# Gathering each expert unit's rows already transposed, with the normed tokens as matmul weights

## What is computed

```python
def grouped_moe(h, router_w, router_b, w_gate, w_up, w_down):
    aff = jax.nn.sigmoid((h @ router_w).astype(jnp.float32))
    ...
    _, idx = lax.top_k(jnp.where(in_group, biased, -jnp.inf), TOP_K)      # 2 of 16
    ...
    for e in range(N_EXPERTS):
        he = jax.nn.silu(h @ w_gate[e]) * (h @ w_up[e])
        y = y + combine[..., e:e + 1] * (he @ w_down[e])
    return y
```

## Time and profile before

| | before |
|---|---|
| median of 3 runs (lowest to highest) | 970.78 us (969.52 to 971.41) |
| profiled execution: span of the core | 969.1 us |
| mean granted TensorE clock in it | 0.906 |
| TensorE matmul busy | 807.4 us (83%) |
| VectorE busy | 405.9 us (42%) |
| ScalarE busy | 178.4 us (18%) |
| HBM read, written | 303.84 MB, 24.12 MB |

### The profile page before, as it was taken

How to read it: one execution, slowest core, us unless ns; L and a number is a source line. 1 busy time by engine, 2 the same in 40 slices (tenths; PEclk the granted TensorE clock), 3 DMA queues, 4 the chain that set the end, 5 groups by cost and what they waited for, 6 DMA issues and landing times.

```text
span 969.1 us, 18246 instructions
## 1 busy us (share of the span) xinstructions
PE 807.4 (83%) x6990; PEld 435.3 (45%) x6991; DVE 405.9 (42%) x944; ACT 178.4 (18%) x383; POOL 43.1 (4%) x71
## 2 busy tenths in 40 slices
PE   8899999997979856996668977799879879697674
PEld 3544646444554423553234543374445535353332
DVE  3267879867879841221011223533522111122315
ACT  3222010325630201111001110330211110111002
POOL 0100000130001010000000001000010000000010
PEclk9799989998999897998778989799899989798878
DMA  9989977999506797859999999994779999999971
GB/s 341 361 305 351 336 266 266 332 347 336 199 1 235 300 404 271 350 223 418 415 418 415 355 406 411 391 416 162 276 293 397 371 414 417 414 417 413 415 302 54
DMA packets 99192, 320.22 MB, mean 330 GB/s; under 512 B 10161, under 2 KB 24417, under 8 KB 82609
## 3 DMA queue, kind: packets, MB, share of 16 engines
q1 hardware_dynamic: 75648, 282.49, 74.3%
q0 software_dynamic: 4864, 22.03, 6.1%
q10 hardware_dynamic: 18624, 14.96, 4.7%
HBM read 303.84 MB, written 24.12 MB: 338 GB/s over the span
## 4 chain that ended last, share of the span: by engine, by line
PE 43%; DMA 25%; DVE 12%; SPq 11%; issue 4%; ACT 3%; ACTq 1%; POOL 1%; DVEq 0%; POOLq 0%
DMA raw<-in_w_up 10%; SPq L479 9%; DMA arena<-unit_rows 9%; PE bank L1824 9%; PE bank L1603 7%; PE bank L1837 4%; PE bank L1593 3%; PE bank L1745 3%; PE bank L1998 3%; PE bank L1607 2%; DMA consts_sb<-in_constants 2%; DMA unit_rows<-arena,row_i 2%; DMA arena<-ada_sums 1%; PE bank L1612 1%; PE bank L1539 1%
## 5 line engine op out<-in xcount | busy, mean ns | idle before, releaser
L1824 PE MATMUL bank<-raw,arena 128*32 128x256 f32 x3392 | 241.8, 428 | 65.2 <-DMA raw<-in_w_up 33.8
L1824 PEld LDWEIGHTS bank<-raw,arena 128*32 128x32 f32 x3392 | 118.0, 121 | 170.0 <-DMA raw<-in_w_up 46.9
L1369 DVE TENSOR_TENSOR arena<-arena,bank 64x256 f32<-64x256 f32 x53 | 22.5, 425 | 340.3 <-ACT arena L815 340.3
L1837 PE MATMUL bank<-raw,arena 128*32 128x256 f32 x1696 | 113.1, 397 | 10.2 <-DVE arena L1357 10.2
L1837 PEld LDWEIGHTS bank<-raw,arena 128*32 128x32 f32 x1696 | 59.6, 115 | 50.1 <-DVE arena L1357 11.1
L1603 PE MATMUL bank<-ring,arena 128*128 128x512 f32 x160 | 69.9, 594 | 0.0
L1811 PE MATMUL bank<-consts_sb,arena 64*128 64x64 f32 x212 | 36.5, 295 | 36.6 <-DVE arena L1369 36.5
L815 ACT ACTIVATE arena<-bank 64x256 f32<-64x256 f32 x53 | 19.9, 376 | 254.5 <-PE bank L1824 217.5
L928 DVE SCALAR_TENSOR_TENSOR bias<-ring,small,bias 128x512 f32<-128x512 f32 x77 | 57.9, 752 | 2.7
L1811 PEld LDWEIGHTS bank<-consts_sb,arena 64*128 64x128 f32 x212 | 29.0, 196 | 48.7 <-DVE arena L1369 41.7
L928 DVE SCALAR_TENSOR_TENSOR arena<-ring,small,arena 128x512 f32<-128x512 f32 x63 | 47.4, 752 | 2.2
(11 more groups left out here) (269 smaller groups left out, 856.4 us busy)
## 6 DMA issues: line engine op xcount, KB each, us to landing
raw<-in_w_gate SPq DMA_DIRECT2D x64, 1024.0 KB, 21.0
raw<-in_w_up SPq DMA_DIRECT2D x64, 1024.0 KB, 23.3
raw<-in_w_down SPq DMA_DIRECT2D x64, 1024.0 KB, 22.3
ring<-in_ada_w SPq DMA_DIRECT2D x24, 2048.0 KB, 13.0
ring<-in_w_in SPq DMA_DIRECT2D x7, 2048.0 KB, 13.2
unit_results<-arena ACTq DMA_DIRECT2D x220, 32.0 KB, 7.2
arena<-unit_rows ACTq DMA_DIRECT2D x55, 128.0 KB, 6.9
ring<-in_w_out SPq DMA_DIRECT2D x2, 2048.0 KB, 42.6
```

Source lines behind the costliest of these rows:

```text
L1824: ins = mm(ps[4][o:o + S, 0:FW], xT[:, i, j * S:(j + 1) * S], w[:, k % 4, h * FW:(h + 1) * FW], start=(k == 0), stop=(k == KD - 1))
L1837: ins = mm(ps[5][j * S:(j + 1) * S, 0:XW], hT_e[:, k % QN, k // QN * S:(k // QN + 1) * S], w[:, k % 2, j * XW:(j + 1) * XW], start=(k == 0 ...
```

## The change

For every unit, TensorE gathers the rows itself and already transposed: for each of the eight blocks of 128 channels it takes the block of `f_` as weights (128 x 128, once for each of the two token tiles) and the unit's selection `chosen` (128 tokens x 32 slots) as moving data. This is 16 matmuls, 32 passes, a unit; the result, `xT`, needs one copy by VectorE. `chosen` is made a unit ahead on VectorE by `choose`, from slot numbers that fall by 32 each time. The list in DRAM, its fills, the scatter, the fetches, ScalarE's copy and the transposes are gone. The gather of unit n + 1 stands between `gate_up(n)` and `down(n - 1)`. As the normed tokens must live until the last unit, the results are fetched into a buffer of closed expert weights. `expert_closed` is signalled by a matmul of one column. The numbers of the result rows are now worked out in `weigh`.

```diff
-                def load_x(n):
-                    act.dma_start(xs[:, 0:XW],
-                                  xg[bass.ds((n + 1) * S, S), :].rearrange("s (j c) -> (s j) c", j=JN)
-                                  ).then_inc(E["x_landed"], 16)
...
                     nc.scalar.activation(sg[64:P, :], ps[4][0:64, 0:FW], ACT.Silu).then_inc(E["silu_done"], 1)
-                    act.wait_ge(E["xT_in_psum"], n + 2)
-                    act.wait_ge(E["x_landed"], n * 16 + 16)
-                    nc.scalar.copy(xs[:, XW:2 * XW], xs[:, 0:XW]).then_inc(E["x_ready"], 1)
-                    act.wait_ge(E["x_ready"], n + 3)
-                    load_x(n + 3)
...
-                act.wait_ge(rows_out, 16 * 2 * TT * (l + 1))
-                load_x(2)
...
-            def send_rows(l):
-                pool.wait_ge(rows_chosen, l + 1)
-                for t in range(TT):
-                    for q in range(2):
-                        pool.indirect_dma_start(xg, bass.IndirectOffsetOnAxis(row_i[:, 2 * t + q:2 * t + q + 1], 0),
-                                                f_[:, t, :], None).then_inc(rows_out, 16)
...
-                        pool.indirect_dma_start(y_of[q][t], None, yg,
+                        pool.indirect_dma_start(y_of[l][q][t], None, yg,
...
+                def choose(n, first=False):
+                    dve.wait_ge(E["ahead_steps"], n * 2 - 3)
+                    nc.vector.tensor_tensor(both, cst("iota")[:, 0:S].rearrange("p (a s) -> p a s", a=1).to_broadcast(
+                        [P, TT * 2, S]), ahead_s.rearrange("p t (q a) -> p (t q) a", a=1).to_broadcast(
+                        [P, TT * 2, S]), ALU.is_equal).then_inc(E["ahead_steps"], 1)
+                    dve.wait_ge(E["ahead_steps"], n * 2 - 2)
+                    nc.vector.tensor_scalar(ahead_s, ahead_s, float(S), None, ALU.subtract
+                                            ).then_inc(E["ahead_steps"], 1)
+                    if not first:
+                        dve.wait_ge(E["x_in_psum"], n)
+                    of_q = both.rearrange("p (t q) s -> p t q s", t=TT)
+                    nc.vector.tensor_tensor(chosen, of_q[:, :, 0, :], of_q[:, :, 1, :], ALU.add
+                                            ).then_inc(E["chosen_ready"], 1)
...
-                def gather(n):
-                    for t in range(TT):
-                        for j in range(JN):
-                            ins = mm(ps[n][j * S:(j + 1) * S, 0:XW], Pg[:, t, n * S:(n + 1) * S],
-                                     f_[:, t, j * XW:(j + 1) * XW], start=(t == 0), stop=(t == TT - 1),
-                                     skip_group_check=True)
-                    ins.then_inc(x_in_psum, 1)
+                def gather(bank, rows):
+                    for k in range(KD):
+                        for t in range(TT):
+                            ins = mm(ps[bank][:, k * S:(k + 1) * S], f_[:, t, k * P:(k + 1) * P], rows[:, t, :],
+                                     start=(t == 0), stop=(t == TT - 1), skip_group_check=True)
+                    ins.then_inc(E["x_in_psum"], 1)
+
+                def gather_ahead(n):
+                    pe.wait_ge(E["chosen_ready"], n - 1)
+                    gather(6, chosen)
...
                     turn_he(n - 1)
                     gate_up(n, own, begins)
+                    gather_ahead(n + 1)
                     down(n - 1, prev)
-                    turn_x(n + 1, begins)
+                    if begins:
+                        close_expert()
...
-                gather(0)
-                gather(1)
-                turn_x(0, False)
+                gather(0, Pg[:, :, 0:S])
...
                 gate_up(0, own, True)
-                turn_x(1, False)
+                gather(6, Pg[:, :, S:2 * S])
...
                     down(n - 1, prev)
                     if i > LATE:
                         scatter(n - 1, False)
+                    close_expert()
                     gate_up(n, own, True)
-                    turn_x(n + 1, True)
+                    gather_ahead(n + 1)
```

More of the change, by code:

```diff
@@ L136 @@
 MAX_UNITS = NE + TT * SEQ // S
+FETCH_AT = [2 * RING + 1, 4]
 LISTED = (MAX_UNITS + 5) * S
@@ L265, in program @@
                           ("slot", (TT, 2)), ("share", (TT, 2)), ("rel", (TT, 2)), ("late_share", (TT, 2)),
-                          ("late_at", (1,))], KD * W + 6 * D + NE * UN)
+                          ("late_at", (1,)), ("row", (TT, 2)), ("ahead", (TT, 2)), ("both", (TT * 2, S)),
+                          ("chosen", (TT, S))], KD * W + 6 * D + NE * UN)
         assert at <= MODS
@@ L270, in program @@
         row_i = placed("row_i", [P, 2 * TT], U32, A0 + KD * W + 6 * D + NE)
-        xs, xT, sg, he, hT_e, gate_s = (me[n] for n in ("xs", "xT", "sg", "he", "hT", "gate"))
+        xT, sg, he, hT_e, gate_s = (me[n] for n in ("xT", "sg", "he", "hT", "gate"))
         lg_part, comb, some, runA, runB, slots, picked, slot_f, share = (me[n] for n in (
             "parts", "comb", "some", "runA", "runB", "slots", "pick", "slot", "share"))
-        rel, late_share, late_at = (me[n] for n in ("rel", "late_share", "late_at"))
+        rel, late_share, late_at, row_f, ahead_s, both, chosen = (me[n] for n in (
+            "rel", "late_share", "late_at", "row", "ahead", "both", "chosen"))
         ys, Pg, Ph = (lay([("ys", (4, XW)), ("Pg", (TT, 2 * S)), ("Ph", (TT, 2 * S))], 2 * D)[0][n]
                       for n in ("ys", "Pg", "Ph"))
-        y_of = ([f_[:, t, :] for t in range(TT)], [bias[:].rearrange("p a n -> p (a n)"), arena[:, 3 * D:4 * D]])
+        fetched0 = [halves[s][:].rearrange("p (t n) -> p t n", t=TT) for s in FETCH_AT]
+        y_of = [([fetched0[l][:, t, :] for t in range(TT)], [bias[:].rearrange("p a n -> p (a n)"),
+                                                            arena[:, 3 * D:4 * D]]) for l in range(2)]
         fT = lay([("fT", (KD, SEQ))], KD * W + 4 * D)[0]["fT"]
@@ L600, in _ @@
                 if c == FILL_AFTER:
-                    for dst, a, b in fills:
-                        pool.dma_start(dst[a:b, :], x[0:b - a, :]).then_inc(rows_filled, 16)
+                    pool.wait_ge(b_ready, 1)
+                    for a, b in fills:
+                        pool.dma_start(yg[a:b, :], x[0:b - a, :]).then_inc(rows_filled, 16)
             load_gain(gmix, 1, 2)
             pool.wait_ge(rows_filled, 16 * len(fills))
-            send_rows(0)
             for b in range(2):
@@ L862, in experts @@
                             late_unit()
-                n = act.snap(units, min_val=NE, max_val=MAX_UNITS)
-                act.wait_ge(E["x_landed"], n * 16 + 16)
             norm2(2, lambda t: act.wait_ge(mix_used, 3 + t))
@@ L1380, in next_unit @@
                     product(n)
+                    turned(n + 1)
                     result(n - 1, place, stores)
-                    turned(n + 1)
+                    choose(n + 2)
                     dve.reg_add(units, units, 1)
```

77 lines of the change are left out of this document (35 added, 42 removed).

## The result

| | us |
|---|---|
| before, median of 4 runs | 971.1 (969.5 to 976.0) |
| after, median of 4 runs | 1099.5 (1090.5 to 1105.9) |
| ratio, 95% interval | 1.132, 1.127 to 1.137: slower |
| profiled execution after: its own time, its span, mean granted clock | 1105.9, 1104.1, 0.893 |
| forecast | 1022 (1004 to 1050) |

The direction was right, and the size was missed by 77 us: the time lies outside the range, where the severe form of rival 3 had put it (1095). From the page of the changed kernel: span, granted clock and GB/s in 40 slices (of 27.6 us), the chain by line, and the gather's two groups (L1791).

The account below looks back on a forecast made before the run. Expert stages were taken as bound by weights in places, elsewhere by TensorE, row fetches and SyncE's queue. Layer 0 +28.7 and layer 1 +22.6 make 51.3; 969.1 + 51.3 + 1.7 = 1022 us, range 1004 to 1050.

Parts of the forecast that it names:

- rival 3: Gathers in the units: few moving columns halve TensorE's clock; some 1095 us, about 1050 if every other unit; chance 0.10.
- The price of a gather: TensorE, each unit: 32 passes bound by loading weights, 0.111 us each, 3.57 us a gather.
- Rival 1: Gather passes on TensorE: cheaper than the weight-load rows, 57 ns each, 1.83 us a gather; 961 us; chance 0.06.
- rival 2: Gather passes on TensorE: load and matmul don't overlap, 0.139 us a pass, 4.4 us a gather; 1062 us; chance 0.07.
- The unit: TensorE, one unit: 6.34 us less 0.37 for the transposes plus 3.57 for the gather, 9.54 us.
- The clock falls: Title of rival 3: half clock for 3.4 us of every unit would add 1.7 us a unit; chance 0.10.
- Layer 0: Layer 0's expert stage: expert 3 +6.1 us, by the end of the layer +28.7 us (+24.3 to +33.0).
- early start: Head of layer 0: unit 1 starts at 361.1 instead of 371.62, 10.5 us earlier.
- Unit 1 as before: Start of layer 1: unit 1 at 706.4 + 7.72 = 714.1, as before to 0.3 us.
- would look alike: Under rival 2: code fetched late for 16 more instructions a unit; a part of it is in the high end, 1050.
- The rest of layer 1: Layer 1 after its start: TensorE bounds throughout; expert 13 +24.7 us, the layer's end +22.6 us.
- DMA and SyncE: DMA queues: row fetches (0.32 us each) and scatter go; list fills, result fetches and SyncE's closed-expert signal cost nothing.

Follow-up runs that it names:

- e2_block: Changed kernel with one of the gather's eight blocks per unit ahead (2 matmuls instead of 16), so its output is incomplete: 954.2 us.
- e_wide: Changed kernel with each gather matmul moving its 32 selection columns four times over, same weight loads and result: 1052.9 us.
- e1_mix: Changed kernel with the same gather matmuls spread through the unit's gate and up matmuls instead of standing in a row: 1116.8 us.
- e6_head: Kernel before, with ScalarE's wait for the scattered rows and first row fetch moved behind unit 0's SiLU, to start unit 1 early: 974.1 us.

## Why the prediction was wrong

Taken step by step, in the prediction's order:

**1. The price of a gather: right.** Forecast 3.57 us and 0.111 us a pass; measured 3.68 (0.115), and 0.112 as the difference to e2_block. Rival 1 (cheaper) and rival 2 (0.139 us) are out. The load of the weights, read from two rows of before, was the right thing to price by. The passes of L1533 would have misled: they took 0.26 us each (16 from 28.12 to 32.21), but their weights are read with a stride of eight (`rows[:, v, k:D:KD]`), and the gather's lie side by side.

**2. The unit: nearly right.** Forecast 9.54 us, measured 9.73, and 9.81 in e_wide. Of the 0.19 us, 0.11 are the gather's price, and 0.11 stand between gate and up and what follows it: 3.59 us from start to start (380.30 to 383.89) where down used to follow after 3.48 (388.04 to 391.52 before), the hand-over to 128-column weights that e1_mix shows. Down takes 0.04 us more and the turn 0.07 less.

**3. The clock: the step that failed.** "The clock falls" had 0.10 because dense matmuls stand before and behind each gather. They do, and the clock fell all the same. The mean granted clock was 0.893 in the changed kernel (1104.1 us) and 0.955 in e_wide (1051.0): 2 x 0.107 x 1104 = 236 us at half clock against 2 x 0.045 x 1051 = 95. Measured cost: 1099.5 - 1052.9 = **46.6 us** (53.1 by the two profiled spans). The warning row was in front of me: in the earlier trace rows a stretch of full weight loads with 2 moving columns, TensorE never idle, is followed by 0.57. I weighed it down by an argument that no row showed. Rival 3 had the mechanism right in kind. That its severe price, 1095 us, came out near the result is luck: it put 73 us on the clock (1095 - 1022), where 46.6 were measured, and the rest comes from steps 4 to 6.

**4. Layer 0, with the clock out of it.** By e_wide the last unit is 647.1 - 608.1 = 39.0 us late, forecast +28.7. Unit 1 of the changed kernel starts at 367.47, forecast 361.1: the stage itself began 4.0 us later than before (the rank matmuls at 347.41 against 343.37), and 1.90 us were a stall put down to nothing. So of the 10.5 us of early start 4.2 were left. The late begin of the stage differs in part from execution to execution: e_wide, the same program up to there, has 345.30; its cause stays open. Part of the delay is absorbed between the layers, where the kernel before waited 1.95 us for the sums from DRAM and e_wide doesn't: gate and up of unit 26 start at 741.99 in e_wide against 706.36 before, 35.6 us late, 6.9 more than forecast.

**5. Layer 1's start: a term that I had at zero.** "Unit 1 as before", then 9.54 us a unit. In e_wide it is 39.6 us from the end of gate and up of unit 26 to that of unit 29; the forecast had 7.72 + 2 x 9.54 = 26.8, so **12.8 us** are missing. Two rows of e_wide hold most of them:

```profile
764.00 4.47 PE L1825 MATMUL bank<-raw,arena 128*32 128x256 f32 x45 [2.49 <-issue]
...
779.45 5.84 PE L1825 MATMUL bank<-raw,arena 128*32 128x256 f32 x55 [3.98 <-issue]
```

The stalls are 6.5 us, and the 100 passes behind them, most of them at half clock, took 10.3 us instead of 5.7. I had named late code for 16 more instructions a unit only as something that "would look alike" under rival 2, and priced it in the range; it is a mechanism of its own. The kernel before passes the like of it behind waits for VectorE and ScalarE; the change took those waits away and lengthened the code (42 fetches of it against 36). For layer 0, e6_head shows a stall of 4.74 us where the wait is gone; for layer 1 it is only argued.

**6. The rest of layer 1.** From unit 29 to unit 52 e_wide loses 78.0 - 51.5 = 26.5 us on the kernel before. The forecast had 22.6, less 3.1 up to unit 29 and 3.0 for the last gather, which stands behind unit 52: 16.5. Of the 10.0 us between them, 19 units that are 0.27 us longer make 5.1, and five stalls put down to nothing (0.23 to 1.13 us, none of which the kernel before has there) 3.1. The other 1.8 us I can't assign.

**7. DMA and SyncE: right.** The row fetches are gone, TensorE bounds both layers where units are many and layer 1 throughout, and e_wide still waits for weights in experts 7 to 10 of layer 0, up to 2.16 us at a time.

In sum, the 77.5 us between forecast and result are 46.6 for the clock, 6.9 up to the start of layer 1, 12.8 in its first units, 10.0 in the rest of it, and about 1 behind the last unit and between span and median.

## What to carry to other kernels

That TensorE is never idle doesn't by itself keep its clock up. In this kernel a row of 32 passes that each load 128 columns of weights and move 32 cost the time of its loads, and also the clock of what stood behind it. Two remedies helped here: to move more columns behind the same load (repeating them cost 0.1 us a unit), and to cut the row in two; in crumbs among matmuls of another weight shape it cost more than it gave. Look at the granted clock of every stretch that gets such a row. Before you count on a wait that the change removes, ask what was hidden behind it, the fetch of the engine's own code among the rest: look for the stalls put down to nothing, and for what the instruction queue brings in them.

## What the runs showed that I had not expected

- Four times the matmul work made the kernel 46.6 us faster: 0.1 us more for each gather, and a granted clock of 1.00 instead of 0.81 to 0.87.
- A hand-over between weights of 32 and of 128 columns costs about 0.1 us each way.
- Later branch marks, with marks for the late experts' branches, cost 50 us (1052.9 to 1103.2), with single stalls of 13.1 us and 70 fetches of code instead of 42.
